# Four weight units of a state space projection recast as seven half-block products between attention steps

## The reference, cut to what matters

```python
proj = h @ w_in
q_lat, kv_lat, k_idx, w_idx, z, xbc, dt_raw, g_a, g_b = jnp.split(proj, IN_SPLITS, axis=-1)
y_a = sparse_mla_attention(q_lat, kv_lat, ...) @ w_o_attn
y_b = ssd_mixer(z, xbc, dt_raw, ...) @ w_o_ssd
...
# ssd_mixer: xbc has 4096 columns; causal convolution of 4 taps over the tokens, one filter per column
xbc = lax.conv_general_dilated(xbc, conv_w[:, None, :], window_strides=(1,),
                               padding=[(CONV_W - 1, 0)], ...) + conv_b
xbc = jax.nn.silu(xbc)
# attention, per head: logits = q kv^T + bias, masked; probs = softmax(logits); out = probs @ kv
```

## Time and profile before

| | |
|---|---|
| time, median of 3 runs | 1331.04 us (1330.92 to 1332.16) |
| the profiled execution, its own time | 1330.91 us |
| its span in the profile | 1329.1 us |
| TensorE matmul busy | 1317.1 us, 99% of the span |
| VectorE, ScalarE, GpSimd busy | 906.9, 404.9, 180.4 us |
| chain that ended last | PE 92%, DVE 4%, DMA 2%, ACT 1%, issue 1% |

### The profile page before, as it was taken

One profiled execution on the slowest core, in us unless ns is written; L12 is line 12 of the kernel. 1 busy time (PEld: TensorE's weight loads), 2 busy tenths in 40 slices (PEclk: granted clock), 3 DMA queues, 4 the chain that ended last, 5 costly groups with the idle time before them and its releaser, 6 DMA issues.

```text
span 1329.1 us, 21123 instructions
## 1 busy us (share of the span) xinstructions
PE 1317.1 (99%) x8749; PEld 1165.2 (88%) x8749; DVE 906.9 (68%) x1558; ACT 404.9 (30%) x881; POOL 180.4 (14%) x167
## 2 busy tenths in 40 slices
PE   9999999999999999999999999999999999999998
PEld 7985899988897599998877888889999986999987
DVE  3974788657587388857863895557887845865653
ACT  2154333230216333322055214444742103100101
POOL 2300322030200032104042000003200100011100
PEclk9999999999999999999999999999999999999999
DMA  9532577676433257756648733037634554545550
GB/s 322 196 127 96 190 257 255 226 270 212 175 110 112 96 210 278 256 208 252 220 90 259 223 127 122 22 118 247 207 128 161 188 185 132 181 144 184 174 174 34
DMA packets 129408, 238.14 MB, mean 179 GB/s; under 512 B 7414, under 2 KB 34318, under 8 KB 128802
## 3 DMA queue, kind: packets, MB, share of 16 engines
q1 hardware_dynamic: 123354, 218.26, 47.7%
q0 software_dynamic: 5552, 18.34, 5.1%
q10 hardware_dynamic: 407, 0.20, 0.1%
HBM read 231.49 MB, written 6.34 MB: 179 GB/s over the span
## 4 chain that ended last, share of the span: by engine, by line
PE 92%; DVE 4%; DMA 2%; ACT 1%; issue 1%; SPq 0%; DVEq 0%
PE acc L2069 58%; PE scr L2069 17%; PE pvw L2069 9%; DMA ring<-in_w_up 1%; PE ptb L2178 1%; PE pvw L2679 1%; PE scr L2672 1%; DMA hid<-in_x 1%; PE ptb L2069 1%; PE scr L2169 1%; DVE ring L1292 1%; PE scr L2650 1%; DVE ring L1232 1%; DVE work L1294 0%; DVE work L1291 0%
## 5 line engine op out<-in xcount | busy, mean ns | idle before, releaser
L2069 PE MATMUL acc<-y,ring 128*128 128x128 f32 (+2 forms) x1216 | 206.3, 325 | 0.0
L2069 PEld LDWEIGHTS acc<-y,ring 128*128 128x128 f32 (+1 forms) x1216 | 182.9, 191 | 17.6 <-issue 1.7
L2069 PE MATMUL acc<-x,ring 128*128 128x128 f32 (+1 forms) x832 | 120.7, 299 | 0.0
L2069 PEld LDWEIGHTS acc<-x,ring 128*128 128x128 f32 x832 | 110.9, 192 | 5.8 <-issue 1.0
L2069 PE MATMUL acc<-ring,big 128*128 128x256 f32 (+1 forms) x376 | 115.5, 453 | 0.0
L2069 PEld LDWEIGHTS acc<-ring,big 128*128 128x128 f32 x376 | 70.6, 190 | 33.3 <-issue 26.9
L2069 PE MATMUL acc<-ring,hid 128*128 128x256 f32 (+1 forms) x364 | 98.8, 417 | 0.0
L871 ACT ACTIVATE ring<-ring,silc 128x512 f32<-128x512 f32 x96 | 60.1, 709 | 92.3 <-DMA ring<-in_ada_w 92.3
L2069 PEld LDWEIGHTS acc<-ring,hid 128*128 128x128 f32 x364 | 68.4, 190 | 21.7 <-issue 14.3
L2069 PE MATMUL acc<-ysq,ring 128*128 128x128 f32 x592 | 71.9, 275 | 0.1
L2069 PEld LDWEIGHTS acc<-ysq,ring 128*128 128x128 f32 x592 | 68.9, 192 | 0.4 <-ACT ysq L1026 0.4
(11 more groups left out here) (548 smaller groups left out, 2627.1 us busy)
## 6 DMA issues: line engine op xcount, KB each, us to landing
ring<-in_w_in SPq DMA_DIRECT2D x24, 2048.0 KB, 9.3
ring<-in_w_up SPq DMA_DIRECT2D x16, 2048.0 KB, 8.7
ring<-in_w_down SPq DMA_DIRECT2D x16, 2048.0 KB, 8.0
ring<-in_ada_w SPq DMA_DIRECT2D x12, 2048.0 KB, 12.8
ring<-in_w_ffn_in SPq DMA_DIRECT2D x22, 1024.0 KB, 7.3
ring<-in_w_out SPq DMA_DIRECT2D x6, 2048.0 KB, 7.9
ring<-in_w_o_ssd SPq DMA_DIRECT2D x4, 2048.0 KB, 7.9
ring<-in_w_ffn_out SPq DMA_DIRECT2D x4, 2048.0 KB, 7.8
```

The source lines that it names most:

```text
L2069: ins = pe.matmul(dst, w, m, start=start, stop=stop, is_transpose=turned, skip_group_check=True)
```

## The change

The first four `xbc` units stay as they are (`b2` = 0 to 7). The last four are done as seven products each, with the four attention slots of a unit placed before, between and inside products. The accumulators `acc0` to `acc3` hold one unit at a time, since `scr` and `pvw` belong to the attention; so a unit's banks are free for the next one only after its combine. Tap 0 of the convolution of these units moves from DVE to ACT (`first_taps`), the copies to `pre` are replaced by the combine, which writes `pre`. POOL's `token_sums2(32, ...)` moves ahead: it now waits for `masked` to reach 4 (the last `mask_bias`), and `sz` lies in `upad`, `kiz`, `st` and `adm`. The small matmuls for `acum` move from before `b2` = 15 to after `b2` = 7. At the start of the kernel one semaphore is replaced by `consts_in`.

On TensorE, for each of the four units:

```diff
+            def half_product(w, a, dst, i, opens):
+                for k in range(4):
+                    ins = mm(dst[:, i * P:(i + 1) * P], w[:, k, i * P:(i + 1) * P], a[:, k, :], opens and i == 0 and k == 0, k == 3)
...
+            def xbc_seven(u):
...
+                first_step = 2 * (2 * FIRST_SEVEN - FIRST2) + 4 * u
+                slot2(first_step)
+                pe.wait_ge(ma_free, group + 2)
...
+                for i in range(2):
+                    half_product(b11, y[:, 0:4, 0:H], acc[0][:, 0, :], i, True)
+                for i in range(2):
+                    ins = half_product(b22, sz[3], acc[0][:, 1, :], i, False)
+                ins.then_inc(ma_full, 1)
+                slot2(first_step + 1)
+                pe.wait_ge(mb_free, group + 2)
...
+                for i in range(2):
+                    ins = half_product(b21, y[:, 4:8, 0:H], acc[1][:, 0, :], i, True)
+                ins.then_inc(gate_pe, 1)
+                pe.wait_ge(t_ready, t_base + 1)
+                pe.wait_ge(mc_free, group + 2)
...
+                half_product(xbc_t1, sz[0], acc[2][:, 1, :], 0, True)
+                slot2(first_step + 2)
+                half_product(xbc_t1, sz[0], acc[2][:, 1, :], 1, False)
+                pe.wait_ge(t_ready, t_base + 2)
+                for i in range(2):
+                    ins = half_product(b12, sz[2], acc[2][:, 0, :], i, False)
+                ins.then_inc(mc_full, 1)
+                pe.wait_ge(t_ready, t_base + 3)
+                half_product(b22, sz[1], acc[1][:, 1, :], 0, False)
+                slot2(first_step + 3)
+                half_product(b22, sz[1], acc[1][:, 1, :], 1, False).then_inc(mb_full, 1)
+                pe.wait_ge(t_ready, t_base + 4)
+                pe.wait_ge(mz_free, group + 1)
+                for i in range(2):
+                    ins = half_product(b21, y[:, 4:8, H:T], acc[3][:, 0, :], i, True)
+                ins.then_inc(mz_full, 1)
...
+            pe.wait_ge(mz_free, XBC_G + SEVEN_XBC + 1)
```

On DVE:

```diff
+            def xbc_combine(u):
...
+                dve.wait_ge(ma_free, before + 3)
+                dve.wait_ge(mb_full, before + 1)
+                tt(pre[:, 0, :, low], by_tile(xbc_first[:, 0, :]), by_tile(acc[1][:, 0, :]), ALU.add)
+                tt(xbc_one, xbc_first[:, 0, :], acc[1][:, 1, :], ALU.add).then_inc(mb_free, 1)
+                dve.wait_ge(mb_free, before + 3)
+                dve.wait_ge(mc_full, before + 1)
+                tt(xbc_pair, xbc_one.unsqueeze(1).broadcast_to([P, 2, T]), acc[2][:, :, :], ALU.add).then_inc(c_step, 1)
+                dve.wait_ge(c_step, 2 * before + 1)
+                tt(pre[:, 1, :, high], by_tile(xbc_pair[:, 0, :]), by_tile(acc[2][:, 1, :]), ALU.add).then_inc(mc_free, 1)
+                tt(pre[:, 1, :, low], by_tile(xbc_pair[:, 1, :]), by_tile(xbc_first[:, 1, :]), ALU.add).then_inc(c_step, 1)
+                dve.wait_ge(mz_full, before + 1)
+                tt(pre[:, 0, :, high], by_tile(xbc_pair[:, 0, :]), by_tile(acc[3][:, 0, :]), ALU.add).then_inc(mz_free, 1)
...
+            for u in range(SEVEN_XBC):
+                for j in range(4):
+                    k = 2 * (2 * FIRST_SEVEN - FIRST2) + 4 * u + j
+                    if k < STEPS2:
+                        logits2(k)
+                    if 0 <= k - 1 < STEPS2:
+                        attention(k - 1)
+                    if j == 0:
+                        xbc_sums(u)
+                    elif j == 1:
+                        if u:
+                            other_taps(u - 1, 0)
+                        else:
+                            conv2(2 * FIRST_SEVEN - 1)
+                    elif j == 2:
+                        xbc_late_sums(u)
+                    else:
+                        if u:
+                            other_taps(u - 1, 1)
+                        xbc_combine(u)
...
             attn_sums(0)
-            conv2(15)
-
-            bank_out(55)
+            for pair in range(2):
+                other_taps(SEVEN_XBC - 1, pair)
+
+            bank_out(47)
```

`xbc_sums` and `xbc_late_sums` are two additions of 128 x 1024 each; `other_taps(u, pair)` is taps 1 to 3 for two column tiles, six instructions like L1606. On ACT `first_taps(u - 1)` (four activations of 128 x 256) stands behind the slot of `j` = 0, the copy of `acc0` behind the slot of `j` = 1, and `first_taps(3)` before the copies of the `w_uv_2` results. On POOL:

```diff
+            pool.wait_ge(h2_ready, DC)
+            pool.wait_ge(i_full, 8)
+            pool.wait_ge(masked, 4)
+            token_sums2(32, y[:, 0:4, 0:H], y[:, 4:8, 0:H], y[:, 0:4, H:T], y[:, 4:8, H:T], *sz)
...
-            pool.wait_ge(h2_ready, DC)
-            pool.wait_ge(i_full, 8)
-            pool.wait_ge(o_full, DEPTH * STEPS + STEPS2)
-            token_sums2(32, y[:, 0:4, 0:H], y[:, 4:8, 0:H], y[:, 0:4, H:T], y[:, 4:8, H:T], *sz)
```

More of the change, by code:

```diff
@@ L267, in build @@
         acumT = work[0:SSD_HEADS, 13, :]
[L268 removed]
+        acum_rows = [[pre[:, 0, :, 0:T], pre[:, 1, :, 0:T]], [pt[:, i].rearrange("p (m a) t -> p m (a t)", m=2) for i in range(2)]]
         xbc = big
@@ L1012, in slot2 @@
                     output_back2(k - 2)
-            for b2 in range(16):
+            for b2 in range(2 * FIRST_SEVEN):
                 if b2 >= FIRST2:
@@ L1023, in _, with first_taps @@
                 copied(pre[:, b2 % 2, :, TAPS2 - 1:], b[:, :, :])
+            copied(acum[:, :, :], full()[:, :, 0:SSD_HEADS])
+            def first_taps(u):
+                act.wait_ge(mz_free, XBC_G + u + 2)
+                for a4 in range(4):
+                    c = 4 * (FIRST_SEVEN + u) + a4
+                    act.activation(xbc[:, c, :], pre[:, a4 // 2, a4 % 2, 0:T], ACT.Identity, scale=pcol[:, 3, c:c + 1],
+                                   bias=pcol[:, 4, c:c + 1]).then_inc(tap_done, 1)
+            for u in range(SEVEN_XBC):
+                for j in range(4):
+                    slot2(2 * (2 * FIRST_SEVEN - FIRST2) + 4 * u + j)
+                    if j == 0 and u:
+                        first_taps(u - 1)
+                    if j == 1:
+                        act.wait_ge(ma_full, XBC_G + u + 1)
+                        act.wait_ge(mz_free, XBC_G + u + 1)
+                        act.activation(xbc_first, acc[0][:, :, :], ACT.Copy).then_inc(ma_free, 1)
+            first_taps(SEVEN_XBC - 1)
             for j in range(4):
@@ new lines, in other_taps @@
+            def other_taps(u, pair):
+                dve.wait_ge(tap_done, 4 * u + 2 * pair + 2)
+                for tap in range(1, TAPS2):
+                    for i in range(2):
+                        c = 4 * (FIRST_SEVEN + u) + 2 * pair + i
+                        if tap > 1:
+                            steps.sync(1)
+                        ins = stt(xbc[:, c, :], pre[:, pair, i, tap:tap + T], pcol[:, 3, 32 * tap + c:32 * tap + c + 1], xbc[:, c, :],
+                                  ALU.mult, ALU.add)
+                        if tap == TAPS2 - 1 and i == 1:
+                            ins.then_inc(pre_used, 1)
+                        else:
+                            steps.mark(ins)
@@ L2680, in values2, with slot2 @@
                 ins.then_inc(o_full, 1)
-            for b2 in range(16):
+            def slot2(n):
+                if n + 1 < STEPS2:
+                    scores2(n + 1)
+                if 0 <= n - 1 < STEPS2:
+                    transposes(n - 1, 2)
+                if 0 <= n - 2 < STEPS2:
+                    values2(n - 2)
+            for b2 in range(2 * FIRST_SEVEN):
                 if b2 % 2 == 0:
                     w = next_unit()
[L2685 to L2690, removed]
                 b = free_bank()
@@ L2695, in _ @@
                     if b2 >= FIRST2:
[L2697 to L2703, removed]
+                        slot2(2 * (b2 - FIRST2) + i)
                     c = 2 * (b2 % 2) + i
@@ L2712, in _ @@
+            for u in range(SEVEN_XBC):
+                xbc_seven(u)
+            pe.wait_ge(ma_free, XBC_G + SEVEN_XBC + 2)
+            pe.wait_ge(mb_free, XBC_G + SEVEN_XBC + 2)
+            pe.wait_ge(mc_free, XBC_G + SEVEN_XBC + 2)
+            pe.wait_ge(mz_free, XBC_G + SEVEN_XBC + 1)
             w = next_unit().rearrange("p k n -> p (k n)")
```

90 lines of the change are left out of this document (67 added, 23 removed).

## The result

The changed kernel takes 1336.23 us in the median of seven runs (1335.09 to 1336.91); the kernel before, beside it, 1331.11 us (1330.92 to 1332.16). The ratio is 1.0033, with an interval of 1.0023 to 1.0042: slower, by 5.1 us, where 4.8 were forecast. The profiled execution took 1336.91 us, its span 1335.1 us.

What follows compares the result with a forecast made beforehand. TensorE, busy 99% of the span, was taken as the bound: 5.1 us gained by the shorter stream, 5.2 lost at hand-overs, 1.2 after the fourth unit, 3.5 at the entry, +4.8 in all, 1335.8 us; range 1331.0 to 1339.0.

Steps and rivals of the forecast that it cites:

- The stream: TensorE, last four units: 13.80 us of tiles replaced by 12.53 us of products each, 5.1 us gained in all.
- The switches: TensorE going from moving 256 to 128 tokens, four times a unit: taken as nothing, at most 0.1 us each, 1.6 in all.
- The hand-over between units: At three borders TensorE's transposes wait for attention weights queued behind VectorE's combine: 1.7 us each, 5.2 us.
- (c): VectorE is in time at every slot, so hand-overs and entry cost nothing: -3.9 us, 1327.1 us, faster; 13%.
- (d): GpSimd's lock delays TensorE at the entry but the hand-overs cost nothing: -0.4 us, 1330.6 us, same; 7%.
- (e): VectorE falls behind inside the units too and the shape switches cost: +8.8 us, 1339.8 us, slower; 13%.
- The entry: Before step 0's transposes, GpSimd's moved sums hold VectorE's taps 4.5 us; less 1.0 slack, TensorE loses 3.5 us.
- a bound of 0.6: At the stage's start, upper bound: 0.6 us on top of 3.5 us if tap 0 waits for GpSimd as well.
- (b): GpSimd's sums wait for VectorE's taps, not the reverse, so the lock spares TensorE: +1.3 us, 1332.3 us, same; 17%.
- After the fourth unit: TensorE waits for the whole combine before `w_uv_2`, net 0.85 us, then 0.3 us for `sattn[0]` at `m5`: 1.2 us.
- Tap 0 on ScalarE: Four activations a unit, at most 2.4 us on ScalarE's 9.03 us, hidden under the unit's 21.2 us.
- The sum: Whole kernel: -5.1 + 5.2 + 1.2 + 3.5 = +4.8 us, 1335.8 us for the median, slower; 50%.

Runs made afterwards that it cites:

- Experiment 2: The changed kernel, but at the three borders between units VectorE makes the next slot's logits and attention weights ahead of the combine: 1331.48 us, ratio 1.0001.
- Experiment 4: The kernel before the change with only GpSimd's input sums moved behind the last mask addition, and the tiles this needs: 1335.16 us, ratio 1.0026.
- experiment 1: The changed kernel, but GpSimd's four input sums also wait for the attention weights of step 0: 1332.69 us, ratio 1.001.
- experiment 5: The changed kernel with tap 0 of the last four units back on VectorE: 1338.8 us; two more profiled runs of it took 1338.16 and 1338.61 us.

## Why the prediction was right, by its own steps

- **The stream**: forecast -5.1, measured -5.15 and +0.1 for `acum`. This fits by luck. The switches, put at nothing, cost the upper bound of 0.1 us each (1.89 for 1.79), 0.4 us a unit, and the slots, put at their old length, gave the same back (2.06 for 2.17). What shrank in a slot is the first step, `scores2` to `transposes`, 0.76 us for 0.86; it now stands behind a product of 128 tokens and no longer behind a tile of 256. 21.2 us a unit was forecast, 21.17 came.
- **The hand-over between units**: forecast three of 1.7, +5.2; measured 1.73 each net, +5.2. Every mark of the count in VectorE's queue stood where it was put: combine at +0.38, `at_ready` at +4.39. On TensorE's side two small errors cancel: the transposes were wanted at +2.55, not +2.65, and started 0.05 after `at_ready`, so the wait was 1.89, of which 0.15 came back in the slot. Experiment 2 shows that nothing else makes the wait. Rivals (c) and (d) fell on this. Inside the units VectorE was in time, which rules out (e).
- **The entry**: forecast +3.5, measured +2.95, right in mechanism and a little large. The stretch of VectorE between the mask's end and `logits2` grew by 4.07 us (7.02 for 2.95) where I had 4.5. I had the taps wait 0.7 + 3 x 1.27 us and tap 0 not at all; in fact the first sum fell beside tap 0, which was held for about 1 us (a case that I kept only as a bound of 0.6), and the taps lost 3.1. Experiment 4 shows the term by itself, experiment 1 shows it gone. Rival (b) fell on this.
- **After the fourth unit**: forecast 0.85 and 0.3, together +1.2; measured 1.16 and 0.05. The combine was done at +2.97, as forecast. What failed is the subtraction of the 0.33 us of idle that stood there before: 0.29 of it came on top of the wait again. The total holds because both parts lead to one mark: `sattn[0]` was ready at 900.81 + 0.68, +12.99, for a forecast of +13.0, and what TensorE lost earlier it did not have to wait for there. `m5` starts 901.56 - 899.72 = 1.84 us behind the product ahead of it, 0.05 over the pace.
- **Tap 0 on ScalarE**: forecast as hidden, and it was; experiment 5 adds that leaving it on VectorE would have cost 1.3 us at the product that needs `sattn`.
- **The sum**: +4.8 forecast, +4.4 measured with the same start; the entry, 0.55 us too high, is the main part of that difference. It is +5.1 between the medians, where most of the other 0.7 is the start.

The Trainium skill, SBUF — State Buffer, section Who interferes with whom, has an instruction with two SBUF inputs contend with GpSimd's reads and block for a whole instruction, not slow down. The trace agrees: six taps 5.49 us, where sharing at half pace would give at most 4.7 for them; when GpSimd's last sum ended, 4.09 us after the first tap began, 795.25 - 793.85 = 1.40 us of taps were still to do, so in those 4.09 us only 0.97 of the 2.37 were done. The same section says that `tensor_scalar` can enter a mode that takes both ports and then contends as well; the held pair of tap 0 (1.60 us) agrees with that, and I had not drawn on it.

## What to carry to other kernels

When a shorter stream removes slack, read the other engine's queue in order and count from the event that starts its long piece of work: a hand-over can be late on an engine that idles 6.5 us just before. The cure is then the order (the small step that another engine needs goes ahead of the combine, into the idle time), which here turned 4.4 us lost into 3.6 gained together with one later start on GpSimd. Place GpSimd's work on SBUF where nothing urgent stands behind VectorE's next instructions: VectorE lost 4.1 us to it in one place and 3.0 in the other (4.71 for the 1.66 that four taps took before), but TensorE lost 3 us in the first and nothing in the second. And before differences of one or two microseconds are put down to an edit, compare the stage's own length: here three places far from the change moved whole runs by as much.

## What the runs showed of the hardware that I had not expected

- A tensor times scalar plus scalar with one tensor in SBUF is held by GpSimd's addition: the pair of 128 x 256 took 1.60 us for 0.65.
- TensorE's granted clock fell to 0.50 (1.2 GHz) behind waits of 1.14 and 2.13 us in two of three profiles of one kernel (experiment 5), and stayed at 1.00 behind the same waits in all three of the changed kernel and in those of experiments 2 and 4. Where it fell it cost 1.4 us beyond the waits.
- At the start of the program four weight loads took 0.87 us in some executions and 0.47 in others of the same kernel (the first four 0.71 in both), with the granted clock shown as 1.00 in both; the scores of the attention half then began 786.31 - 784.69 = 1.6 us later.
